# Even mixer of a diffusion trunk: order of the softmax, banks of projections and mod groups, and the work behind the scan levels

## What is computed

```python
def even_mixer_context(h, w_in, w_out, lb, gnorm):
    a_q, a_ff, a_fb, a_i, a_g, b_q, b_k, b_v = split_even(h @ w_in)
    o_a, s_fin = hgrn2_mixer(a_q, a_ff, a_fb, a_i, a_g, lb, gnorm, s0)
    o_b = context_attention(q, k, v)
    out = concatenate([o_a, o_b]) @ w_out        # and s_fin, k, v are outputs

def hgrn2_forget(z, lb):
    f = lb + (1.0 - lb) * sigmoid(z)
    k = (1.0 - lb) * sigmoid(-z)

def chunk_scan(q, k, v, log_f, s0):              # forward and backward, 4 heads
    o = (att, masked by decay) @ v + (q * exp(b)) @ S
    S = exp(b_end) * S + (k * exp(b_end - b)).T @ v
```

## Time and profile before

| what | value |
|---|---|
| time, median of 3 | 1718.84 us (1717.68 to 1720.63) |
| the profiled execution | 1717.6 us, span 1715.4 us |
| PE busy | 1634.6 us, 95% |
| DVE busy | 833.5 us, 49% |
| ACT busy | 694.0 us, 40% |
| GpSimd busy | 55.3 us, 3% |
| chain that ended last | PE 82%, DVE 10%, issue 4%, ACT 3%, DMA 2% |
| HBM read | 256.56 MB, 151 GB/s over the span |

### The profile page before, as it was taken

How to read it: one execution, slowest core, us unless ns; L and a number is a source line. 1 busy time by engine, 2 the same in 40 slices (tenths; PEclk the granted TensorE clock), 3 DMA queues, 4 the chain that set the end, 5 groups by cost and what they waited for, 6 DMA issues and landing times.

```text
span 1715.4 us, 27668 instructions
## 1 busy us (share of the span) xinstructions
PE 1634.6 (95%) x11325; PEld 1592.0 (93%) x11325; DVE 833.5 (49%) x1313; ACT 694.0 (40%) x1198; POOL 55.3 (3%) x50
## 2 busy tenths in 40 slices
PE   4999999999888989999999999999999999999997
PEld 3999999998767988999999899999989998999997
DVE  1534434464434988543434643443463676443333
ACT  2433333354442436533334543333353355333332
POOL 2000000010110020000000000000000000000000
PEclk8899999999999989999999999999999999999998
DMA  9534456676877124433334533436354266333310
GB/s 331 189 125 134 132 192 222 206 214 166 233 208 244 46 79 155 142 123 126 126 122 135 178 123 125 135 107 221 123 172 148 99 221 197 123 122 124 122 49 37
DMA packets 255919, 260.51 MB, mean 152 GB/s; under 512 B 6625, under 2 KB 253826, under 8 KB 255826
## 3 DMA queue, kind: packets, MB, share of 16 engines
q1 hardware_dynamic: 249664, 251.67, 45.3%
q0 software_dynamic: 1184, 3.11, 1.8%
q10 hardware_dynamic: 4978, 4.41, 0.8%
HBM read 256.56 MB, written 2.62 MB: 151 GB/s over the span
## 4 chain that ended last, share of the span: by engine, by line
PE 82%; DVE 10%; issue 4%; ACT 3%; DMA 2%; SPq 0%; DVEq 0%; ACTq 0%
PE bank L399 23%; PE bank L401 23%; PE bank L400 23%; PE bank L1404 2%; DMA RAW<-in_mod_w 2%; DVE X L1019 1%; DVE HL L985 1%; PE bank L1427 1%; ACT WH L352 1%; DVE MIX L1241 1%; DVE OUTF L1015 1%; DVE WL L366 1%; DVE MIX L1244 1%; PE bank L420 1%; PE bank L421 1%
## 5 line engine op out<-in xcount | busy, mean ns | idle before, releaser
L366 DVE TENSOR_TENSOR WL<-RAW,WH 128x1024 fp32r<-128x1024 f32 (+1 forms) x331 | 396.8, 1200 | 743.9 <-ACT WH L352 743.6
L352 ACT ACTIVATE WH<-RAW 128x1024 fp32r<-128x1024 f32 (+1 forms) x344 | 358.3, 1045 | 702.2 <-PE bank L401 672.5
L399 PE MATMUL bank<-HH,WH 128*128 128x384 f32 x1664 | 562.7, 338 | 2.2 <-ACT MIX L643 2.2
L401 PE MATMUL bank<-HH,WL 128*128 128x384 f32 x1664 | 560.5, 337 | 0.0
L400 PE MATMUL bank<-HL,WH 128*128 128x384 f32 x1664 | 560.4, 337 | 0.0
L399 PEld LDWEIGHTS bank<-HH,WH 128*128 128x128 f32 x1664 | 314.0, 189 | 4.5 <-ACT MIX L643 2.6
L400 PEld LDWEIGHTS bank<-HL,WH 128*128 128x128 f32 x1664 | 313.8, 189 | 0.0
L401 PEld LDWEIGHTS bank<-HH,WL 128*128 128x128 f32 x1664 | 313.7, 189 | 0.0
L399 PE MATMUL bank<-AH,WH 128*128 128x384 f32 x704 | 237.3, 337 | 0.0
L400 PE MATMUL bank<-AL,WH 128*128 128x384 f32 x704 | 236.6, 336 | 0.0
L401 PE MATMUL bank<-AH,WL 128*128 128x384 f32 x704 | 236.6, 336 | 0.0
(11 more groups left out here) (213 smaller groups left out, 1472.6 us busy)
## 6 DMA issues: line engine op xcount, KB each, us to landing
RAW<-in_ffn_w_in SPq DMA_DIRECT2D x88, 1024.0 KB, 5.1
RAW<-in_mod_w SPq DMA_DIRECT2D x72, 1024.0 KB, 6.8
RAW<-in_ffn_w_out SPq DMA_DIRECT2D x32, 1024.0 KB, 5.3
RAW<-in_ab_w_in SPq DMA_DIRECT2D x16, 1024.0 KB, 9.9
RAW<-in_ffn_w_out SPq DMA_DIRECT2D x16, 768.0 KB, 4.7
RAW<-in_cv_w_in SPq DMA_DIRECT2D x12, 1024.0 KB, 5.5
RAW<-in_ab_w_out SPq DMA_DIRECT2D x4, 1024.0 KB, 13.2
RAW<-in_cv_w_out SPq DMA_DIRECT2D x4, 1024.0 KB, 5.4
```

The source lines that it names most:

```text
L352: e.activation(WH[:, (2 * m + b) % 4, 0:nk, :], RAW[:, p, 0:nk, b * P:(b + 1) * P], ACT.Copy).then_inc(half_hi, 1)
L366: e.tensor_tensor(WL[:, k, 0:nk, :], RAW[:, p, 0:nk, b * P:(b + 1) * P], WH[:, k, 0:nk, :].bitcast(F32), ALU.subtract).then_inc(half_ready, 1)
L399: e.matmul(out, WH[:, k, kk, :], xh(kk), start=(first and kk == 0), stop=False)
L401: mm = e.matmul(out, WL[:, k, kk, :], xh(kk), start=False, stop=(last and kk == nk - 1))
```

## The change

The change is to the program of the even mixer on PE, ACT, DVE and GpSimd; no arithmetic changes.

- **Attention steps.** ACT copies the probabilities of u-2 before it takes the exponential u. The weight splits and copies of the projections move from even to odd steps, on ACT and on DVE, so one step behind their projection. Mod columns leave in steps 8, 12, ... and rows in steps 5, 9, ...; the mod turn moves from steps 4, 8, ... to 6, 10, .... The sigmoids move to steps 8 and 16, the gates to 10, 12 and 14 (18, 20 and 22).
- **Banks.** The groups of modC alternate between banks 2 and 3 (before: all in 3), the projections 12 to 23 between 0 and 1 (before: 0, 1, 2).
- **Diagonals.** ACT copies the diagonal scores, not DVE.
- **Behind the levels.** PE turns the keys of two heads in banks 5 and 6 and interleaves, per head, the inner products of the output (VT, ATT), the states in banks 4 and 7, and the next turning. ACT copies the keys first and HH behind them; DVE makes the states first, HL behind them, and then the four low halves that GpSimd had.

```diff
-MOD_BANK = [7, 6, 7, 3, 2, 6, 3, 3, 3, 3, 3, 3, 6, 6, 7, 6, 0, 6]
+MOD_BANK = [7, 6, 7, 3, 2, 6, 2, 3, 2, 3, 2, 3, 6, 6, 7, 6, 0, 6]
-            return bank[tau % 4 if tau < 12 else tau % 3 if tau < 24 else 4 + tau % 4]
+            return bank[tau % 4 if tau < 12 else tau % 2 if tau < 24 else 4 + tau % 4]
...
-            pool.wait_ge(lvl_q, 3 * LEVELS)
-            first_splits("out1")
...
@@ ACT, attention steps
-                        if u >= 4:
-                            act.wait_ge(p_turned, u - 3)
-                    if step % 4 == 1 and step > 1:
-                        mod_cols_out(g0 + step // 4 - 1)
-                    if step % 4 == 0 and step > 0:
+                    if step % 4 == 0 and step >= 8:
+                        mod_cols_out(g0 + step // 4 - 2)
+                    if step % 4 == 1 and step >= 5:
                         mod_rows_out(g0 + step // 4 - 1)
-                    if step < 24 and step % 2 == 0:
+                    if step < 24 and step % 2 == 1:
                         proj(12 + step // 2)
-                    if step in (7, 15):
-                        gate_sigmoids(step // 8)
+                    if step in (8, 16):
+                        gate_sigmoids(step // 8 - 1)
...
+                    if lv == 0:
+                        act.wait_ge(v_stored, 16)
+                        for j in range(3):
+                            act.wait_ge(diag_mm, j + 1)
+                            act.activation(ATT[:, 4 * j:4 * j + 4, :].rearrange("p u t -> p (u t)"), bank[j][:],
+                                           ACT.Copy).then_inc(diag_out, 1)
+                        mod_cols_out(g0 + 5)
...
@@ DVE, attention steps
-                    if step < 24 and step % 2 == 0:
+                    if step < 24 and step % 2 == 1:
                         proj(12 + step // 2)
-                    if step in (9, 17):
+                    if step in (10, 18):
...
@@ DVE, behind the levels
-                for ht in range(4):
-                    cat_lo(ht)
-
...
+                for ht in range(4):
+                    cat_lo(ht)
+                for j in range(4):
+                    split_dve(dve, f"out{s}", j // 2, 8)[j % 2]()
...
@@ PE
-                        pe.wait_ge(proj_out, tau - 2 if tau in range(15, 24) else tau - 3)
+                        pe.wait_ge(proj_out, tau - 1 if tau in range(14, 24) else tau - 3)
...
-                    if step % 4 == 0 and step > 0:
+                    if step % 4 == 2 and step >= 6:
                         mod_turn(g0 + step // 4 - 1)
...
+                turn_keys(0)
+                turn_keys(1)
+                for h in range(HEADS_A):
+                    inside(h)
+                    states(h)
+                    if h < 2:
+                        turn_keys(h + 2)
                 for h in range(HEADS_A):
                     pe.wait_ge(st_ready, 4 * h + 4)
...
```

More of the change, by code:

```diff
@@ L791, in even @@
                         act.activation(SQ[:, u % 2, 0:n], bank[6][:, 0:n], ACT.Copy).then_inc(p_copied, 1)
+                    u = step
+                    if u < 24:
+                        act.wait_ge(s_max, 2 * u + 2)
+                        n = P if u % 3 == 0 else NT
+                        act.activation(TT[:, u % 4, 0:n], bank[4 + u % 2][:, 0:n], ACT.Exp,
+                                       bias=SMALL[:, 0, u % 4:u % 4 + 1], scale=DH ** -0.5,
+                                       accum_out=SMALL[:, 1, u % 4:u % 4 + 1]).then_inc(s_exp, 1)
                     u = step - 3
@@ L1257, in even @@
                     dve.wait_ge(st_mm, h + 1)
-                    B = bank[3 + h % 2]
+                    B = bank[(4, 7)[h % 2]]
                     for w in range(2):
@@ L1701, in head_stat @@
                     pe.matmul(cols3(bank[h]), ONES[:], SQ[:, h % 2, :], start=True, stop=True).then_inc(o_stat, 1)
+                pe.wait_ge(mod_cols, first_group("modD"))
+                turn_keys(0)
[5 more added lines that the diff above has]
+                        turn_keys(h + 2)
                 for h in range(HEADS_A):
                     pe.wait_ge(st_ready, 4 * h + 4)
-                    O = bank[h]
-                    for t in range(TOKS):
-                        out = O[:, t * P:(t + 1) * P]
-                        terms = [(VT[:, t, h * P:(h + 1) * P], ATT[:, TOKS * h + t, :])]
-                        if t > 0:
-                            first = (ST[:, h, :], KFW[:, h, P:2 * P])
-                            last = (ST[:, 4 + h, :], KBW[:, h, P:2 * P])
-                            terms.append((first[t - 1], QF[:, h, t * P:(t + 1) * P]))
-                            terms.append((last[2 - t], QB[:, h, t * P:(t + 1) * P]))
-                        for n, (l, r) in enumerate(terms):
-                            mm = pe.matmul(out, l, r, start=(n == 0), stop=(n == len(terms) - 1))
+                    for t in (1, 2):
+                        out = bank[h][:, t * P:(t + 1) * P]
+                        first = (ST[:, h, :], KFW[:, h, P:2 * P])
+                        last = (ST[:, 4 + h, :], KBW[:, h, P:2 * P])
+                        pe.matmul(out, first[t - 1], QF[:, h, t * P:(t + 1) * P], start=False, stop=False)
+                        mm = pe.matmul(out, last[2 - t], QB[:, h, t * P:(t + 1) * P], start=False, stop=(t == 2))
                     mm.then_inc(o_mm, 1)
```

61 lines of the change are left out of this document (26 added, 35 removed).

## The result

The changed kernel takes **1704.87 us** in the median (1697.99 to 1714.1, 9 runs), the kernel before, beside it, 1717.68 (1715.38 to 1720.63, 9 runs). The ratio is 0.9926, 95% interval 0.9905 to 0.9946: faster by 12.8 us (9.3 to 16.3), where 9.0 were forecast. The profiled execution took 1704.91 us with a span of 1703.1. PE is busy 96% of it, and the chain that ended last is 83% PE, with DMA now at 4% instead of 2%.

What follows compares the result with a forecast made beforehand. TensorE, busy 95%, was taken as the bound, with loads next. Gains of 2.6 us in attention and 6.4 behind the levels, 9.0 in all, gave 1709.8 us; range 1695 to 1718.

Steps and rivals of the forecast that it cites:

- Part 1: Attention softmax chain: moving splits behind the exponential removes 6.7 us of turning waits for SQ; sigmoids and gates covered.
- Part 2: Attention steps, two banks each: 8.5 us of mod column waits and 3.6 of row waits go; projections cost nothing.
- The loads: Attention mod pairs: later splits delay load bursts, new waits on tiles of 18.2 us, bounds 12.6 and 24.
- The rule of the Trainium skill: DMA engines alternate between queues per packet, so bias loads take their share anywhere; would make the kernel 1712.3 us.
- group 3: Mod tile loads with the bias load ahead of the burst: landing 10.1 us taken, wait 4.3.
- Slow work: Attention, PE working slowly and small gaps: 8.0 us before, 7.3 after in proportion to waits, bounds 2 and 10.
- The ideal of 116.7: Attention stage without waits, added up from step parts that ran freely: 116.7 us, against 144.8 measured before.
- Part 3: Diagonal score copies moved from DVE to ACT: cost nothing, covered by a projection; some 2 us if uncovered.
- Part 4: Behind the levels: GpSimd no longer slows DVE, states end at 618, gain 6.4 us, bounds 3.4 and 7.4.
- Sum: Attention 2.6 plus behind the levels 6.4 gives 9.0 us gained, median 1709.8.
- (a): Rival: loads keep up in the attention steps, which gain 26.1 us; total 1686, chance 0.09.

Runs made afterwards that it cites:

- the two other executions of the same code: The changed kernel run again, 1705.74 us; and the changed attention steps with the old part behind the levels, 1709.13 us.
- late pairs: Changed kernel with PE's mod pairs one odd step later, turn, rows and columns two steps later, all loads kept: 1684.67 us, ratio 0.9809 to the kernel before.
- half of the loads: Changed kernel with 4 of 8 k tiles loaded for each modC tile, PE's matmuls kept: 1686.99 us, ratio 0.9815 to the kernel before.
- GpSimd's rest alone: Kernel before with only GpSimd's four weight subtractions behind the levels moved to DVE, behind the states: 1712.75 us, ratio 0.9970.

## Why the prediction was right, and where its steps were not

The forecast was 1709.8, the result 1704.87, within the range. The mechanisms stood: better order and banks move the bound to the loads, and GpSimd at rest frees DVE. That the sum came so near was partly luck: by the medians of the parts alone the attention gave 8.6 us (5.7 to 10.3) where 2.6 were forecast, and the part behind the levels 2.5 (0.9 to 5.7) where 6.4 were.

- **Part 1.** Right: of the 6.7 us that the turning waited for SQ nothing is left, and the sigmoids and gates cost nothing seen. The burst of step 9 began at 438.72, 5.0 us behind the score of step 7 (433.75); 5.1 had been forecast.
- **Part 2.** Undervalued. The MOD and ROWS waits went as forecast, but I gave the banks no sum of their own. Alone they win 12.8 us of median (1719.9 to 1707.14, ratio 0.9928), attention 139.7.
- **The loads.** 11.5 us of waits on tiles against 18.2 forecast, but 14.8 and 17.5 in the two other executions of the same code. Steps 5, 13 and 17 came as forecast: 1.35, 4.65 and 1.80 us against 1.5, 4.3 and 1.5. Step 9, 6.9 forecast, had 0, 3.18 and 6.12. The landing was well sized where the bias load came soon: in the second and third execution the second tile landed 12.5 and 13.4 us behind the start of the burst, against 12.7; in the first, with the bias load 4.1 us behind, 8.5. The step that failed is PE's way there: 5.8 us behind the burst for a PE without waits, but it came 12.7, 9.5 and 7.5 us behind, since I looked only at each group's first pair. Steps 7 and 19 wait 2.19 and 1.53 us for the fourth tile, which landed 17.1 us after its issue at 419.96 and 16.8 after that at 494.66, and PE works slowly behind. Step 21, 4.0 forecast, waited for nothing (0.7 and 1.1 in the others) for the same reason.
- **The rule of the Trainium skill** that was weighed ("DMA: Bandwidth & Descriptors", Queues, rings and completion order) would by the forecast's rows have made 6.8 us for group 3; the trace has 4.65, with the bias load issued at 460.55, 4.1 us ahead of the burst, and the other two have 4.70 and 4.83. Here the bound in between was nearer, and the second tile landed 10.1 us behind the start of the burst, as taken. That a bias load takes time from the tiles agrees with the run without bias loads: 6.4 us less attention.
- **Slow work.** 140.3 - 116.7 - 13.1 (the tile waits and 1.6 of two others) = 10.5 us, not 7.3; in the other two executions 7.5 and 5.9. The proportion to the waits is not seen: less slow work went with more waits. Waits and slow work together were 23.6, 23.9 and 25.0 us, against 25.5 forecast. The ideal of 116.7 did hold, to about 1 us: late pairs took 120.1 with 2.2 of waits for DVE and 0.8 of issue and one mod turn (0.5) less in the steps, and half of the loads 119.5 with 3.6 of waits.
- **Part 3.** No cost on the critical path by the rows, but the stretch from the diagonals to the keys grew by 1.9, which nothing in the sum foresaw. The diagonal matmuls took 4.90 us instead of 2.9. In the second run of the changed kernel they took 2.92, behind the same waits of 1.0 and 0.6, and the stretch 62.5, as before; so this belongs to that execution and is no price of ACT's copies. A slow clock fits it (0.87 from 540 to 560, 1.00 in the second run).
- **Part 4.** 5.8 us in the trace against 6.4. The cause was right and is shown: GpSimd beside DVE. From the turning of the keys the states took 9.3 us (614.8 - 605.55), not 8.1 (618 - 609.9). A head comes every 2.0 us on PE, in the middle of the 1.3 to 2.6 assumed, but by luck. The sum took the eight records of a head's state products for eight matmuls, where they are four, and so counted 11 pieces a head where the trace has 18 (4, 6 and 8); and PE's clock was 1.00 there, for which the sum had 1.3 us. DVE's eight operations behind them took 6.3, not 6.8. The sum also gave the interleaving a part in the gain, and it brings 0.3. In medians the part shows less: 1715.23 against 1717.77 alone. The interval ends at 5.7, and the same gain of the trace with GpSimd's rest alone shows 5.0 in the median. Whether the interleaving gives some of it back further on stays open.
- **Sum.** 4.5 + 5.8 = 10.3 against 9.0, less 1.9 and with the 3.9 in untouched code makes the 12.3 of the spans.
- **Rivals.** (a), that the loads keep up, did not come: waits on tiles and slow work stayed. Late pairs shows that its time was well sized: 0.9809 of the forecast's 1718.84 is 1686.0, and (a) said 1686.

## What to carry to other kernels

When a wait is removed by moving a step back, look at what that step frees: here the weight split frees a load slot, and a better order of the chain was worth 11 us in the attention steps only once the consumer of the loads stood one step later. A wait on a DMA in a ring is a loop (late data, late consumer, late slot, late load), so one step of slack for the consumer can bring as much as half of the bytes (120.1 against 119.5 us here). Cost every tile of a burst, the last one above all, and carry a wait that you forecast on to when the next one begins. Read a stage twice before trusting 2 us of it: the wait of one step was 0, 3.2 and 6.1 us in three executions of the same code.

## What the runs showed of the hardware

- Four DVE subtractions of 128x384 take 8.41 us beside GpSimd's subtractions and 1.96 alone, and the two operations of 128x8 ahead of them 2.56 and 0.37. So GpSimd's 10.30 us of work cost DVE 8.6 us, 6.45 of it in the subtractions.
- Bias loads in rows of 256 bytes, 1.18 MB, took 16.0% of the DMA engines' time in 141 us, six times as much a megabyte as the weights; without them the attention steps were 6.4 us shorter. How late they make a tile depends on their distance: issued 0.8, 2.9 and 4.1 us behind the start of a burst, they went with 13.0, 12.1 and 8.1 us to landing for its second tile.
- PE after a wait of 1.5 to 4.7 us for a tile did 64 small matmuls in 3.4 to 3.6 us instead of 1.95, three times of five, with a granted clock of 0.59 and 0.65 in the windows behind two of them. Over the three executions of this code it followed each of the five longest waits (3.18 to 6.12 us) and three of the fourteen shorter ones (0.72 to 2.20). Late pairs had no wait for a tile and a clock of 1.00 in the windows shown, one of them with loads at 340 GB/s, so busy loads alone don't slow PE. What it is in a wait that does was not tried.
- In one queue 1 MB tiles landed 5.1 us (the first), 7.7 (the second), 10.9 (the third) and 17.1 us (the fourth) after their issues at 417.56 to 419.96: the last tile of a burst takes three times as long as its first.
